# Low parts of the down projection's token blocks: seven on VectorE, or five on GpSimd and two on VectorE

## The reference

```
h = _rms_norm(x, g_ffn)
u = square(relu(h @ w_up))      # 2048 -> 8192
y = x + u @ w_down              # 8192 -> 2048
```

## Time and profile before

| | us |
|---|---|
| median of 3 runs (3226.42 to 3229.4) | 3228.12 |
| the profiled execution | 3228.48 |
| its span, first to last instruction | 3226.9 |
| PE busy, share of the span | 3066.0 (95%) |
| DVE busy | 2272.1 (70%) |
| ACT busy | 1579.8 (49%) |
| POOL busy | 373.6 (12%) |

### The profile page before, as it was taken

One profiled execution on the slowest core, in us unless ns is written; L12 is line 12 of the kernel. 1 busy time (PEld: TensorE's weight loads), 2 busy tenths in 40 slices (PEclk: granted clock), 3 DMA queues, 4 the chain that ended last, 5 costly groups with the idle time before them and its releaser, 6 DMA issues.

```text
span 3226.9 us, 65154 instructions
## 1 busy us (share of the span) xinstructions
PE 3066.0 (95%) x23991; PEld 2921.9 (91%) x23991; DVE 2272.1 (70%) x3071; ACT 1579.8 (49%) x2170; POOL 373.6 (12%) x655
## 2 busy tenths in 40 slices
PE   6999999999999999989789979999999898999999
PEld 5999999999999998867359869999999898989999
DVE  4225666665555557899863398888888988888876
ACT  4224666665555556777752244444444434343533
POOL 1111111111111113233310000000000000000000
PEclk9999999999999999999999989999999999999999
DMA  6434333333334337799983435555545745363543
GB/s 188 118 105 111 95 106 99 107 109 94 105 99 112 90 96 249 277 325 339 349 307 93 125 94 151 151 152 150 151 150 153 257 113 176 107 191 106 185 113 92
DMA packets 561257, 499.09 MB, mean 155 GB/s; under 512 B 21304, under 2 KB 489272, under 8 KB 556232
## 3 DMA queue, kind: packets, MB, share of 16 engines
q1 hardware_dynamic: 513024, 349.55, 36.9%
q0 software_dynamic: 48096, 147.75, 13.3%
HBM read 439.63 MB, written 57.57 MB: 154 GB/s over the span
## 4 chain that ended last, share of the span: by engine, by line
PE 84%; DVE 9%; DMA 2%; ACT 2%; issue 2%; POOL 0%; SPq 0%; POOLq 0%; ACTq 0%; DVEq 0%
PE ps L921 25%; PE ps L922 24%; PE ps L923 24%; PE ps L1104 3%; DVE b_lo L1801 2%; DVE w_lo L1801 2%; PE ps L1115 2%; PE ps L1116 2%; PE ps L1037 2%; DVE pg_lo L1801 1%; DMA pg<-in_cache_fox_v_dram 1%; DMA w_raw<-in_w_out_dram 1%; DMA w_raw<-in_cache_fox_v_dram 1%; PE ps L1146 1%; PE ps L1147 1%
## 5 line engine op out<-in xcount | busy, mean ns | idle before, releaser
L921 PE MATMUL ps<-b_hi,w_hi 128*128 128x260 f32 x3584 | 1017.9, 284 | 61.7 <-DVE b_lo L1801 31.2
L922 PE MATMUL ps<-b_hi,w_lo 128*128 128x260 f32 x3584 | 1014.6, 283 | 0.0
L923 PE MATMUL ps<-b_lo,w_hi 128*128 128x260 f32 x3584 | 1014.1, 283 | 0.0
L921 PE MATMUL ps<-h_hi,w_hi 128*128 128x260 f32 (+1 forms) x2592 | 748.7, 289 | 15.9 <-DVE h_lo L1801 12.8
L921 PEld LDWEIGHTS ps<-b_hi,w_hi 128*128 128x128 f32 x3584 | 676.8, 189 | 68.2 <-issue 34.4
L922 PE MATMUL ps<-h_hi,w_lo 128*128 128x260 f32 (+1 forms) x2592 | 736.1, 284 | 0.0
L923 PE MATMUL ps<-h_lo,w_hi 128*128 128x260 f32 (+1 forms) x2592 | 735.4, 284 | 0.0
L923 PEld LDWEIGHTS ps<-b_lo,w_hi 128*128 128x128 f32 x3584 | 678.3, 189 | 0.0
L922 PEld LDWEIGHTS ps<-b_hi,w_lo 128*128 128x128 f32 x3584 | 677.5, 189 | 0.0
L1801 DVE TENSOR_TENSOR w_lo<-w_raw,w_hi 128x1024 fp32r<-128x1024 f32 (+1 forms) x321 | 495.7, 1544 | 240.0 <-ACT w_hi L1348 188.1
L921 PEld LDWEIGHTS ps<-h_hi,w_hi 128*128 128x128 f32 x2592 | 489.9, 189 | 19.4 <-DVE h_lo L1801 14.3
(11 more groups left out here) (301 smaller groups left out, 4644.0 us busy)
## 6 DMA issues: line engine op xcount, KB each, us to landing
w_raw<-in_w_in_dram SPq DMA_DIRECT2D x81, 1024.0 KB, 5.7
w_raw<-in_w_up_dram SPq DMA_DIRECT2D x112, 512.0 KB, 4.1
w_raw<-in_w_down_dram SPq DMA_DIRECT2D x112, 512.0 KB, 4.6
u_dram<-x2T POOLq DMA_DIRECT2D x32, 910.0 KB, 4.9
b_lo<-u_dram SPq DMA_DIRECT2D x28, 1040.0 KB, 9.8
pg<-in_cache_sb_v_dram POOLq DMA_DIRECT2D x106, 256.0 KB, 4.9
w_raw<-in_cache_fox_k_dram SPq DMA_DIRECT2D x72, 256.0 KB, 5.3
w_raw<-in_w_out_dram SPq DMA_DIRECT2D x16, 1024.0 KB, 5.9
```

The lines of the kernel that those rows point to most:

```text
L921: pe.matmul(out, whi, xhi, start=first, stop=False, skip_group_check=more)
L922: pe.matmul(out, wlo, xhi, start=False, stop=False, skip_group_check=more)
L923: return pe.matmul(out, whi, xlo, start=False, stop=last, skip_group_check=more)
```

## The change

Blocks 0, 1, 2, 4 and 6 get their low part from a `tensor_tensor` subtract on POOL, and 3 and 5 from DVE as before. POOL counts them on the semaphore `masks`, which stands at 12 from the program's start; the product of each slot waits for the engine that makes its block. POOL's instructions stand behind its stores: the first three of the first chunk ahead of the store of the last pair, the others behind it.

```diff
+POOL0 = 12
+POOL_LOW = (0, 1, 2, 4, 6)
+DVE_LOW = (3, 5)
...
+        blk_pool = masks
...
-            with pool.Fori(1, NU // 2) as j:
+            with pool.Fori(1, NU // 2 - 1) as j:
                 for p in range(2):
                     store(Pair(p, j, 2))
+            store(Pair(NU - 2))
+
+            def block_low(c, i):
+                pool.wait_ge(blk_hi, count(c, 7, i + BLK0 + 1))
+                pool.tensor_tensor(b_lo[:, i, :, :], b_raw[:, i, :, :], b_hi[:, i, :, :].bitcast(F32),
+                                   ALU.subtract).then_inc(blk_pool, 1)
+
+            for k in range(NC):
+                for i in POOL_LOW[:3]:
+                    block_low(Pair(k), i)
+                if k == 0:
+                    store(Pair(NU - 1))
+                for i in POOL_LOW[3:]:
+                    block_low(Pair(k), i)
...
                 if fresh is not None:
-                    pe.wait_ge(blk_lo, count(fresh, 7, AT[o] + BLK0 + 1))
+                    i = AT[o]
+                    if i in POOL_LOW:
+                        pe.wait_ge(blk_pool, count(fresh, len(POOL_LOW), POOL_LOW.index(i) + POOL0 + 1))
+                    else:
+                        pe.wait_ge(blk_lo, count(fresh, len(DVE_LOW), DVE_LOW.index(i) + BLK0 + 1))
...
             def block_low(c, i):
+                if i in POOL_LOW:
+                    return
                 dve.wait_ge(blk_hi, count(c, 7, i + BLK0 + 1))
                 minus(b_lo[:, i, :, :], b_raw[:, i, :, :], b_hi[:, i, :, :]).then_inc(blk_lo, 1)
```

## The result

The changed kernel took 3275.66 us (median of 3 runs, 3272.64 to 3278.58) against 3228.12 before: a ratio of 1.0148 (95% interval 1.0125 to 1.0171). It is 1.5% slower, and the forecast was 3274. Its profiled execution took 3272.64 us, with a span of 3271.1.

The account below looks back on a forecast made before the run. PE bounds mid-chunk and DVE the four chunk starts, where PE waits 32.3 us in all. From 3228.5 us, 5 x 4.5 us held less 11.2 us removed, four times, adds 45: 3274 us, range 3256 to 3287, 8 in 10 from 3200.

Parts of the forecast that it names:

- Removed: At each chunk start five block lows leave DVE, 5 x 2.24 = 11.2 us of its time.
- the sum: Added to the profiled execution: 5 x 4.5 - 11.2 = +11.3 us a chunk start, four of them +45, so 3274 us.
- POOL's op: Five POOL subtracts of 128x2080 a chunk start, taken at 4.9 us each, between 1.8 and 9.8.
- POOL's queue: Three POOL blocks ahead of the last store, issued at 2537.53, would delay it by a few us and change nothing.
- PE's wait for POOL: At a chunk start PE's third product would wait 3.0 us for POOL's third block; 3.0 of 8.1 us come back.
- What POOL's reading does to DVE: At chunk starts DVE's two-operand instructions lose nothing, or stand while POOL's runs: 0 to 4.9 us a block.
- the upper end: For DVE's loss at chunk starts: held for most of POOL's instruction, 4.5 us a block, given 50%.
- h: Microseconds of DVE's time lost to one POOL block at a chunk start, taken as 4.5.
- The clock: After longer PE waits, one half-speed product a chunk start may show: up to +10 us, kept for the range's upper end.
- The markers: Signs of a held DVE: longer rows or unnamed gaps, PE's list naming DVE with some 78 us, half-speed stretches at four starts.
- the break-even: At chunk starts PE's wait is unchanged if a POOL block costs DVE 2.24 us, what the block costs DVE now.

Follow-up runs that it names:

- the memsets: In the changed kernel, three memsets replaced each POOL subtract, the five blocks' low parts left out: 3212.41 us, ratio 0.9946 to the kernel before.
- copy: In the changed kernel, a one-operand copy of the raw block replaced each POOL subtract: 3217.31 us, ratio 0.9963 to the kernel before.

## Why the prediction was right

*Removed.* 11.2 us a chunk start, and 3196 at best: the kernel without the five lows took 3197.17. That DVE would then stop nobody was not quite right: 7.8 us of waits stayed, and 5.6 us of faster matmuls, for which the sum had no term, made up for most of them.

*POOL's op.* Taken at 4.9 us; the 20 average 5.44 us with their own waits for DVE in them, and the shortest took 4.67.

*POOL's queue.* The last store was issued at 2540.44 in place of 2537.53, and PE's list has no wait that names it.

*PE's wait for POOL.* The 3.0 us a start did not come, 1.1 us in all did, because the held DVE was later still. Where DVE ran free beside an equally long POOL instruction (the memsets), PE's waits came to 18.7 us, near the 19.2 of the same working, though half of them name a weight low that was done at the same moment.

*What POOL's reading does to DVE.* This was the step that decided, and the upper end was right. It was chosen by argument, at a chance of about one in two; no row of before had POOL reading beside DVE, and the experiments are what shows it. The size was a little off: 129 x 0.20 + 110 x 0.21 + 18 x 0.93 + 18 x 0.73 + 17 x 0.26 = 83 us of stretch over the usual 1.22 us (0.42 for the last group), so h = 83 / 20 = 4.2 us, where 4.5 stood. The sum by that is 4 x (20.8 - 11.2) = +38 us, and PE's waits grew by 71.0 - 32.3 = 38.7. The Trainium skill's rule ("SBUF — State Buffer", Who interferes with whom) agrees with all of it: reads hold (subtract, copy), writes don't (memset), an operand from PSUM isn't held, and an instruction is held to the other's end.

*The clock.* Here the sum was too small: I counted nothing and kept 10 us for the upper end. PE's busy time grew from 3066.0 to 3077.5 us, 11.5 us, and 11.1 of that in the same 5551 matmuls of the last stage (673.0 to 684.1 us). The granted clock was 0.87 over a chunk start's 65 us, where it had been 1.00 over the same stretch before (2678 to 2743 us). Waits and slow matmuls together make 38.7 + 11.5 = 50.2 us; the profiled executions differ by 44.2. In the changed one the first token low part, far ahead of the change, started 5.7 us earlier (1855.8 against 1861.5 us), which leaves 0.3 us. So the hold was sized 7 us too high and the clock 11 us too low. The two errors work against each other, so that the forecast missed by only 2 us is in part luck. The clock's share rests on these rows; no run changed the clock alone.

*The markers.* PE's list was to name DVE with some 78 us. It names DVE with 49.0 and nobody with 20.9. DVE's rows were to grow or gaps to open; they grew. The half-speed stretches came.

None of these kernels points to a version faster than the kernel before that computes the same: each column that POOL subtracts costs DVE more (4.2 us a block) than DVE's own subtract (2.24 us).

## What to carry to other kernels

Before work that reads SBUF is moved from DVE to POOL beside a busy DVE, compare POOL's whole instruction, less what it overlaps of DVE's idle time, with what DVE spends on the same work: here 4.2 against 2.24 us, and the break-even tells the sign. A hold is no idle time in the profile; it shows as a single instruction of several times its usual length, and a group's mean hides it unless the count beside it is read. And a longer wait of PE can be paid twice, once as the wait and once in half-speed matmuls behind it: here 38.7 and 11 us.

## What the runs showed of the hardware beyond that

- POOL's copy of 128x2080 from f32 to fp32r took 2.47 us on average (shortest 1.92), under half of the subtract's 5.44 (shortest 4.67), and its memset of the same block 1.84 us.
- The exclusion works in both directions: cutting POOL's instruction in four moved most of PE's waiting from DVE (49.0 us by name before the cut, 12.8 after it) to POOL (1.1 and 49.6), at the same time within 0.1%.
- Waits of PE of 6 to 11 us left the granted clock at 0.50 for the next product, with matmuls 0.22 us apart, where they are 0.12 us apart at full clock.
